# Value products of the attention as three fp32r products each, and VectorE's softmax steps in another order

## What is computed

```python
# branch a: 16 heads of 128, 4 key/value heads
s = einsum('bnkgd,bmkd->bkgnm', qg, k) * (d ** -0.5)
p = softmax(s)
o = einsum('bkgnm,bmkd->bnkgd', p, v)
# branch b: 8 heads, two score maps of 64 each, one value head of 128 each
p = softmax(einsum('bnhid,bmhid->bhinm', q, k) * (dh ** -0.5))
a = p[:, :, 0] - lam * p[:, :, 1]
o = einsum('bhnm,bmhe->bnhe', a, v)
```

## Time and profile before

| | |
|---|---|
| median of 3 runs | 2879.66 us (2878.16 to 2880.67) |
| the profiled execution | 2878.6 us |
| its span | 2877.0 us |
| PE busy | 2850.1 us (99%) |
| DVE busy | 1979.0 us (69%) |
| ACT busy | 1340.1 us (47%) |
| attention rounds, first to last transposes | 1629.5 to 1887.2 us |

### The profile page before, as it was taken

How to read it: one execution, slowest core, us unless ns; L and a number is a source line. 1 busy time by engine, 2 the same in 40 slices (tenths; PEclk the granted TensorE clock), 3 DMA queues, 4 the chain that set the end, 5 groups by cost and what they waited for, 6 DMA issues and landing times.

```text
span 2877.0 us, 34986 instructions
## 1 busy us (share of the span) xinstructions
PE 2850.1 (99%) x13743; PEld 2371.8 (82%) x13743; DVE 1979.0 (69%) x2561; ACT 1340.1 (47%) x1687; POOL 23.5 (1%) x47
## 2 busy tenths in 40 slices
PE   9999999999999999999999999999999999999999
PEld 8988788888888887788888788788878888888887
DVE  6876699999877668866647766667675555655444
ACT  5545554444444447532334655544454444444333
POOL 2000000000000000000000000000000000000000
PEclk9999999999999999999999999999999999999999
DMA  7545587878878877556646534358757777776664
GB/s 249 143 123 162 177 257 250 257 249 251 257 248 270 271 258 248 153 156 192 179 138 188 154 118 122 113 169 263 228 170 238 221 226 226 225 227 198 190 192 152
DMA packets 299955, 583.25 MB, mean 203 GB/s; under 512 B 18393, under 2 KB 18801, under 8 KB 299152
## 3 DMA queue, kind: packets, MB, share of 16 engines
q1 hardware_dynamic: 296896, 572.01, 64.2%
q0 software_dynamic: 2320, 7.96, 0.9%
q10 hardware_dynamic: 576, 1.05, 0.1%
HBM read 578.85 MB, written 2.10 MB: 202 GB/s over the span
## 4 chain that ended last, share of the span: by engine, by line
PE 94%; DVE 3%; ACT 1%; issue 1%; DMA 0%; SPq 0%; ACTq 0%; DVEq 0%
PE psum L565 22%; PE psum L568 22%; PE psum L567 22%; PE psum L634 3%; PE psum L632 3%; PE psum L633 3%; PE psum L2976 2%; PE psum L2978 2%; PE psum L2977 2%; PE psum L513 2%; PE psum L515 1%; PE psum L516 1%; PE psum L3008 1%; PE psum L2996 1%; PE psum L593 1%
## 5 line engine op out<-in xcount | busy, mean ns | idle before, releaser
L697 DVE TENSOR_TENSOR w_lo<-w_raw,w_hi 128x1024 fp32r<-128x1024 f32 x720 | 877.9, 1224 | 579.9 <-ACT w_hi L691 575.9
L691 ACT ACTIVATE w_hi<-w_raw 128x1024 fp32r<-128x1024 f32 x720 | 762.8, 1060 | 1034.5 <-PE psum L568 1024.8
L565 PE MATMUL psum<-w_hi,x_split 128*128 128x512 f32 x1912 | 751.2, 393 | 1.2 <-DVE region_b L2317 1.0
L568 PE MATMUL psum<-w_hi,x_split 128*128 128x512 f32 x1912 | 745.7, 390 | 0.0
L567 PE MATMUL psum<-w_lo,x_split 128*128 128x512 f32 x1912 | 745.4, 390 | 0.0
L568 PEld LDWEIGHTS psum<-w_hi,x_split 128*128 128x128 f32 x1912 | 359.6, 188 | 75.5
L565 PEld LDWEIGHTS psum<-w_hi,x_split 128*128 128x128 f32 x1912 | 359.8, 188 | 75.1 <-issue 2.1
L567 PEld LDWEIGHTS psum<-w_lo,x_split 128*128 128x128 f32 x1912 | 359.9, 188 | 72.9
L565 PE MATMUL psum<-w_hi,hidden_split 128*128 128x512 f32 x704 | 274.9, 391 | 0.0
L568 PE MATMUL psum<-w_hi,hidden_split 128*128 128x512 f32 x704 | 274.0, 389 | 0.0
L567 PE MATMUL psum<-w_lo,hidden_split 128*128 128x512 f32 x704 | 273.9, 389 | 0.0
(11 more groups left out here) (381 smaller groups left out, 3598.4 us busy)
## 6 DMA issues: line engine op xcount, KB each, us to landing
w_raw<-in_w_in SPq DMA_DIRECT2D x216, 512.0 KB, 3.7
w_raw<-in_w_ada SPq DMA_DIRECT2D x192, 512.0 KB, 4.8
w_raw<-in_w_ffn_up SPq DMA_DIRECT2D x176, 512.0 KB, 4.5
w_raw<-in_w_ffn_down SPq DMA_DIRECT2D x88, 512.0 KB, 5.6
w_raw<-in_w_ff_gate SPq DMA_DIRECT2D x88, 512.0 KB, 4.3
w_raw<-in_w_ff_up SPq DMA_DIRECT2D x88, 512.0 KB, 4.1
w_raw<-in_w_ff_down SPq DMA_DIRECT2D x88, 512.0 KB, 4.8
w_raw<-in_w_out SPq DMA_DIRECT2D x64, 512.0 KB, 4.8
```

The costliest lines, as they stand in the source:

```text
L565: nc.tensor.matmul(to, x_hi[:, tokens], hi, start=u == 0 and t == 0, stop=False, skip_group_check=True)
L568: mm = nc.tensor.matmul(to, x_lo[:, tokens], hi, start=False, stop=end and t == 1, skip_group_check=True)
L691: nc.scalar.activation(w_hi[:, b.slot(n)], raw[:, b.raw_slot(k)], ACT.Copy).then_inc(w_rounded, 1)
L697: nc.vector.tensor_tensor(w_lo[:, slot], raw[:, b.raw_slot(k)], r(w_hi[:, slot]), ALU.subtract).then_inc(w_split, 1)
```

## The change

**Values as three products.** `values(hd)` becomes twelve fp32r matmuls of 256 columns instead of four fp32 ones. For that the value tile is split: `v_high` on ACT rounds it into `VH` (two buffers, one for each branch), `v_low` on DVE subtracts and writes the remainder over the tile itself. It is done once for each value tile: 8 of branch b and 4 of branch a, in even rounds. The turned probabilities are split as well: ACT rounds bank 6 into `PTS[:, 0]`, and DVE (`turned_low`, once in each of the 48 rounds) subtracts that from bank 6 into `PTS[:, 1]`. `pt_ready` now comes from DVE. `PTS` has one buffer where `PTT` had two, so ACT waits in each round from 2 on for the values of the head before.

**Order on PE.** `values(rd/2 - 1)` stands ahead of the gate units of its round, right behind the transposes.

**Order on DVE.** `probabilities(rd)` comes first in the round, then `maxima(rd + 2)` instead of `maxima(rd + 1)`. `turned_low` comes at the end of the round, ahead of `output`.

The rest renames semaphores (`k_turned` and `q_turned` become one `head_turned`, with counts that go on, and so on), which changes no wait.

```diff
             def values(hd):
-                kind, h = HEADS[hd]
-                j = 4 + h // 4 if kind == "a" else 16 + h
                 pe.wait_ge(S("pt_ready"), 2 * hd + 2)
+                pe.wait_ge(S("v_split"), v_count(hd))
                 if hd >= 1:
                     pe.wait_ge(S("o_ready"), hd)
                 for c in range(4):
-                    mm = nc.tensor.matmul(PS[:, 7, 0:L], KV[:, j, c * P:c * P + P], PTT[:, hd % 2, c],
-                                          start=c == 0, stop=c == 3, skip_group_check=True)
+                    keys = slice(c * P, c * P + P)
+                    v_hi, v_lo = VH[:, v_buffer(hd), keys], KVR[:, v_tile(hd), keys]
+                    nc.tensor.matmul(PS[:, 7, 0:L], v_hi, PTS[:, 0, c], start=c == 0, stop=False, skip_group_check=True)
+                    nc.tensor.matmul(PS[:, 7, 0:L], v_lo, PTS[:, 0, c], start=False, stop=False, skip_group_check=True)
+                    mm = nc.tensor.matmul(PS[:, 7, 0:L], v_hi, PTS[:, 1, c], start=False, stop=c == 3,
+                                          skip_group_check=True)
...
                 ins.then_inc(S("p_turn"), 1)
+                if rd % 2 == 0 and rd >= 2:
+                    values(rd // 2 - 1)
                 for n in gate_units(rd):
                     gate_unit(n)
...
-                if rd % 2 == 0 and rd >= 2:
-                    values(rd // 2 - 1)
...
+            def v_high(hd):
...
+                if hd >= 2:
+                    act.wait_ge(S("pv_done"), hd - 1)
+                nc.scalar.activation(VH[:, v_buffer(hd)], KV[:, v_tile(hd)], ACT.Copy).then_inc(S("v_hi"), 1)
...
+                if rd % 2 == 0 and v_new(rd // 2):
+                    v_high(rd // 2)
                 act.wait_ge(S("p_turn"), rd + 1)
-                if rd >= 4:
-                    act.wait_ge(S("pv_done"), rd // 2 - 1)
-                nc.scalar.activation(PTT[:, (rd // 2) % 2, :, qb * P:(qb + 1) * P],
+                if rd >= 2:
+                    act.wait_ge(S("pv_done"), rd // 2)
+                nc.scalar.activation(PTS[:, 0, :, qb * P:(qb + 1) * P],
                                      PS[:, 6, :].rearrange("p (c q) -> p c q", c=4),
-                                     ACT.Copy).then_inc(S("pt_ready"), 1)
+                                     ACT.Copy).then_inc(S("pt_hi"), 1)
...
+            def v_low(hd):
+                dve.wait_ge(S("v_hi"), v_count(hd))
+                v = v_tile(hd)
+                nc.vector.tensor_tensor(KVR[:, v], KV[:, v], r(VH[:, v_buffer(hd)]), ALU.subtract
+                                        ).then_inc(S("v_split"), 1)
+
+            def turned_low(rd):
+                dve.wait_ge(S("pt_hi"), rd + 1)
+                tokens = slice(rd % 2 * P, rd % 2 * P + P)
+                nc.vector.tensor_tensor(PTS[:, 1, :, tokens], PS[:, 6, :].rearrange("p (c q) -> p c q", c=4),
+                                        r(PTS[:, 0, :, tokens]), ALU.subtract).then_inc(S("pt_ready"), 1)
...
             for rd in range(len(ROUNDS)):
-                if 0 < rd < len(ROUNDS) - 1:
-                    maxima(rd + 1)
                 if rd > 0:
                     probabilities(rd)
+                if rd + 2 < len(ROUNDS):
+                    maxima(rd + 2)
                 for n in gate_units(rd - 1):
                     gate_lo(n)
...
+                if rd % 2 == 0 and v_new(rd // 2):
+                    v_low(rd // 2)
+                turned_low(rd)
                 if rd % 2 == 1 and rd >= 3:
                     output(rd // 2 - 1)
```

More of the change, by code:

```diff
@@ L285, in build @@
             KVR = freed("kv_split", [P, 24, 2 * L], F32R)
+        with nc.sbuf_tensor("pad_t", [P, 20480], F32):
+            PTS = freed("pt_split", [P, 2, 4, L], F32R)
         BF = sb("region_b", [P, NB])
@@ L289, in build @@
             PSP = freed("p_split", [P, 2, 2, L], F32R)
+            VH = freed("v_hi", [P, 2, 2 * L], F32R)
         EV = sb("evac", [P, 2, NF, L])
@@ L602, in build @@
                 KV_FREED[_j, _k] = by, _n[by]
+        KV_FREED_BY = _n
         def kv_freed(eng, j, k):
@@ L1241, in scored, with v_tile, v_buffer, v_new @@
             return JOBS[2 * hd + 1][-1] + 1
+        def v_tile(hd):
+            kind, h = HEADS[hd]
+            return 4 + h // 4 if kind == "a" else 16 + h
+        def v_buffer(hd):
+            return 1 if HEADS[hd][0] == "a" else 0
+        def v_new(hd):
+            kind, h = HEADS[hd]
+            return kind == "b" or h % 4 == 0
+        V_SPLITS = [hd for hd in range(len(HEADS)) if v_new(hd)]
+        def v_count(hd):
+            return max(V_SPLITS.index(x) + 1 for x in V_SPLITS if x <= hd and v_tile(x) == v_tile(hd))
         def o_split_to(q):
@@ L1570, in kv_late @@
                 if u == 6:
-                    act.wait_ge(S("k_turned"), i + 1)
+                    act.wait_ge(S("head_turned"), i + 1)
                     for f in range(4):
-                        nc.scalar.activation(KV[:, 4 * (j - 1) + f], PS[:, 4 + f, :], ACT.Copy).then_inc(S("k_out"), 1)
+                        nc.scalar.activation(KV[:, 4 * (j - 1) + f], PS[:, 4 + f, :], ACT.Copy).then_inc(S("head_out"), 1)
             def q_copy(b, j, n):
                 if j == 0:
-                    act.wait_ge(S("k_turned"), 3)
+                    act.wait_ge(S("head_turned"), 3)
                 elif j >= 2:
-                    act.wait_ge(S("q_turned"), j - 1)
+                    act.wait_ge(S("head_turned"), 3 + j - 1)
                 nc.scalar.activation(KT_TOK[:, 2 * (j % 2)], PS[:, 2 * b.set(j), :], ACT.Copy).then_inc(S("q_half"), 1)
@@ L1601, in q_out @@
             def q_out(g):
-                act.wait_ge(S("q_turned"), g + 1)
+                act.wait_ge(S("head_turned"), 3 + g + 1)
                 nc.scalar.activation(Q[:, NF * g:NF * g + NF], BACK if g < 5 else BACK_Q,
-                                     ACT.Copy).then_inc(S("q_out"), 1)
+                                     ACT.Copy).then_inc(S("head_out"), 1)
             def k_high(hd):
-                act.wait_ge(S("k_out"), 12)
+                act.wait_ge(S("head_out"), 12)
                 if hd >= 2:
@@ L1614, in q_high @@
             def q_high(hd):
[L1615 removed]
+                act.wait_ge(S("head_out"), 12 + q_tile(hd) // NF + 1)
                 if hd >= 2:
@@ L2927, in kv_late @@
                     if i > 0:
-                        pe.wait_ge(S("k_out"), 4 * i)
+                        pe.wait_ge(S("head_out"), 4 * i)
                     for f in range(4):
@@ L2932, in kv_late @@
                                                       KT_TOK[:, (c + 2) % 4, f * P:f * P + P], ident)
-                    ins.then_inc(S("k_turned"), 1)
+                    ins.then_inc(S("head_turned"), 1)
             kv_stream(pe, lambda i: turn_scaled(pe, "norm1", ZT1, i), kv_late)
             def q_turn(g):
-                pe.wait_ge(S("q_roped"), g + 1)
+                pe.wait_ge(S("head_roped"), 3 + g + 1)
                 if g > 0:
-                    pe.wait_ge(S("q_out"), g)
+                    pe.wait_ge(S("head_out"), 12 + g)
                 else:
-                    pe.wait_ge(S("k_out"), 12)
+                    pe.wait_ge(S("head_out"), 12)
                 to = BACK if g < 5 else BACK_Q
@@ L3013, in _ @@
             gate_unit(1)
-            pe.wait_ge(S("q_out"), 5)
+            pe.wait_ge(S("head_out"), 12 + 5)
             pe.wait_ge(evacuated, PHASES["q"].group(5) + 3)
@@ L3022, in _ @@
             gate_unit(5)
-            pe.wait_ge(S("q_out"), 6)
+            pe.wait_ge(S("head_out"), 12 + 6)
             for rd in range(len(ROUNDS)):
```

20 lines of the change are left out of this document (10 added, 10 removed).

## The result

| | before | after |
|---|---|---|
| median of 6 runs each | 2878.72 us (2875.58 to 2880.67) | 2891.09 us (2890.1 to 2893.81) |
| the profiled execution, and its span | 2878.6, 2877.0 us | 2893.8, 2892.2 us |
| first to last transposes | 257.39 us | 268.99 us |

The change makes the kernel slower by 0.4%: ratio 1.0043, interval 1.0034 to 1.0053, 12.4 us by the medians. The profiled execution of the changed kernel is the slowest of its six runs, and the two profiled executions lie 15.2 us apart: 11.6 us between the transposes of round 0 and of round 47, 2.1 us behind them, and 1.5 us ahead of them, in a phase that the change leaves alone.

What follows compares the result with a forecast made beforehand. PE was taken as the bound, with DVE already level at b rounds. Stalls of 14.6 us less 6.7 us saved gave +7.9 us on 2878.6, so 2886.5, as a median 2887.6; range 2878 to 2892.

Steps and rivals of the forecast that it cites:

- C: Rival for the whole kernel: PE's stalls are as worked out, 2887.6 us, from 2883 to 2891; chance 0.58.
- Part 1, the products: `values` on PE: twelve products in steps of 0.12 us save 0.28 us a head, 6.7 us over 24 heads.
- Part 2, the splits: `turned_low` and `v_low` take 0.60 us each of DVE's queue, PSUM costs nothing extra; ACT's added copies cost nothing.
- Part 3, the lists: Attention rounds: DVE's serial list outlasts PE's before the next transposes in some rounds, adding 14.6 us of stalls.
- the first rounds and the rest: Stalls in the first rounds, those with a `gate_keep` and round 32: 0 to 0.7 us each, taken as 1.5 together.
- A stall on PE is not won back: Claim that PE's added stalls count in full, since later phases stand at the same 99%.
- Part 4, the rest: Values ahead of the gate units on PE wait for nothing new; no transfer moves; cost nothing.
- The sum: Whole kernel: 14.6 - 6.7 = +7.9 us on 2878.6 us gives 2886.5, as a median 2887.6.
- Rival A: DVE's additions fit into its idle time, only PE's saving is left: -6.7 us, 2873.0; chance 0.10.
- Rival D: Stalls on PE are longer, 20 us, 2893; or the 192 ns weight load does not hide, 2908; chance 0.10.
- no reserve for what must be done late: DVE's idle time, 87.5 us, lies early in the round before the gate subtraction and can't serve late work.

Runs made afterwards that it cites:

- the first experiment: Against the changed kernel, the second gate units of rounds 4 and 22 moved to rounds 5 and 23; 2885.29 us, ratio 1.002.
- The last experiment: Changed kernel with second gate units redealt; on DVE, gate subtractions before maxima in even rounds, `v_low` and `output` before maxima in odd rounds; 2871.65 us, ratio 0.997.

## Why the prediction was right, and by how much it was off

The sign, the mechanism and the range held: 2891.09 us against 2887.6, in a range that ends at 2892. The time lies at the upper edge, 0.1 us beyond the 2883 to 2891 given for C itself, and for causes that the sum did not have. Step by step:

- **Part 1, the products.** Steps of 0.12 us and even rounds of 5.31 us (8 and 20), where 5.32 was worked out. The kernel with the products alone ran 4.4 us shorter in the rounds. The 23 heads in that time are worth 6.4 us; stalls of 0.8, 0.5 and 0.3 us that came with it at rounds 1, 3 and 42 leave 4.9, and 0.5 us are not found.
- **Part 2, the splits.** 0.60 us a subtraction in DVE's queue was shown by the difference of 0.59 to 0.61 us between stalls with and without `turned_low`. PSUM as an operand cost nothing: `turned_low` takes 684 ns in the mean, and so does `v_low`, which has both in SBUF.
- **Part 3, the lists.** Stalls added, forecast and measured by the distances of starts:

| rounds waited for | forecast | measured |
|---|---|---|
| 6, 24 | 4.4 | 2.14 + 2.13 = 4.27 |
| 12, 42 | 2.2 | 0.84 + 1.85 - 0.71 = 1.98 |
| 19, 31, 37 | 2.5 | 3 x 0.89 = 2.67 |
| 28, 40 | 1.1 | 2 x 0.66 = 1.32 |
| 16 | 1.4 | 1.62 |
| 46 | 1.5 | 1.54 |
| the first rounds and the rest | 1.5 | 1.74 - 0.95 + 0.46 = 1.25 |
| sum | 14.6 | 14.65 |

Each row is good to 0.25 us. That the sum is closer still is luck in part: errors of both signs cancel, and the 1.5 for the first rounds and the rest was a lump estimate.

- "A stall on PE is not won back" is where it was off. It is worse than that: **a stall of 2.1 us can cost 1.6 us more**, since the clock fell behind it. The sum had no term for the clock, which took 3.2 us of the profiled execution; the first experiment takes away the two stalls and the two half-clock stretches together. In other runs it can be less, as the four runs with DVE's old order show.
- **Part 4, the rest**, gave `values(23)` a price of nothing. It waited 1.31 us for DVE's last `output`, and 2.1 us were lost behind round 47 in all. I had followed the lists from transposes to transposes and stopped at the last ones. That ACT's additions cost nothing held: no stall of the transposes is released by it. Within DVE's lists ahead of rounds 16 and 42 there are waits of 0.87 and 0.75 us for a rounding on ACT, for which the prediction had gone above the plain lists there.
- **The sum.** 14.65 - 6.4 (the 23 heads between T0 and T47) + 3.2 = 11.4 of the 11.6 us measured in the rounds, and 2.1 behind them. The remaining 1.5 us of the profiled execution lie ahead of the rounds, where its trace has a half-clock stretch of 3.4 us at 225 us, in a phase that no edit touches. By medians the loss is 12.4 us against the 7.9 forecast.
- Rival A was decided by the point named for it: the probabilities came after PE's 3.95 us. Rival D's first half, longer stalls, is near in size, but by another way than it said: the stalls were not longer, the clock behind them was lower. Its second half, steps of 0.19 us, did not come.

Two statements ahead have to be put right. The granted clock of the kernel before is at its full level through the attention rounds, but not throughout: behind them, where PE does products of one column, stands this window:

```profile
1900.40:1907.00 6.60, 6.60 (x19) 5.34 (x19) 0.73 (x1) 0.29 (x1) 0.00 (x0) 0.50 0.52 166
```

And I called DVE's idle time "no reserve for what must be done late". The last experiment shows that it can be made one, by the order of its list and by the rounds in which gate units lie.

**What stays open.** Values behind the gate units with both split halves double buffered was not tried, nor was each order alone in the kernel before; so of the 5.7 us of the orders, what belongs to PE's order and what to DVE's is not told apart. That the values ahead of the gate units take away the time in which ACT and DVE worked on the next gate split is argued from the lists; with the splits in, DVE's old order gave no better time, which fits it. Why a wait of 2.07 us left the clock alone and those of 1.97 and 1.96 us did not, and why one run of the same kernel keeps the full clock, is open too.

## What to carry to other kernels

When an engine at 65% feeds one at 99%, write both lists between two hand-overs side by side, round by round, and take the sum of the positive differences; the shares of busy time hide it, and here each row of this sum was good to 0.25 us. Before moving work to another engine or giving up an exact operation, deal the movable work anew: here the same instructions took 2891 us or 2872 us by their order alone. Before giving subtractions to GpSimd, look at what VectorE does beside them. Follow the list to the last consumer behind the loop, and price a stall of 2 us or more on TensorE above its own length: in the profiled executions four of five had the clock fall with them.

## What the runs showed of the hardware

- **The clock behind a stall.** In the profiled executions, stalls of 2.14 and 2.13 us inside dense work were each followed by 3.4 us at a granted 0.50, and one of 2.34 us too; with one of 3.04 us the clock was at 0.50 for 6.8 us, the first 0.9 of them still in the stall. One of 2.22 us, and all of 1.85 us or less, had none (all by the distance of starts). It is not the same in every run: with DVE's old order one of four ran at a mean granted 1.000, the others at 0.996 and 0.997.
- **The step of fp32r products with 256 columns** is 0.12 us in the rounds too, with weights that change each time, and 0.21 us at half the clock.
- **GpSimd beside VectorE.** Fp32 subtractions of 128 x 256 and 128 x 512 took GpSimd 0.74 and 1.29 us where nothing held them, against 0.42 and 0.68 on VectorE. Where GpSimd's and VectorE's ran at the same time on operands in SBUF, each waited for the other to end: VectorE's gate subtraction took up to 2.33 us instead of 1.22, its scaling up to 1.43 instead of 0.49, GpSimd's up to 1.66 and 2.28. VectorE's subtraction with an operand in PSUM kept its 0.68.
